# FFN gain applied behind the gather, and layer 1's embedding rows transposed earlier as filling

## The chip, the cores and the metric

The kernel runs on one core of one Trainium2 chip. The metric is the device time of one execution in microseconds. A core has TensorE (matrix products and transposes, PE in the profile, its weight loads PEld), VectorE (DVE), ScalarE (ACT), GpSimd (POOL), SyncE (SP, which issues most transfers) and 16 DMA engines. Each engine runs its own list of instructions in order; semaphores join the lists.

## The reference, cut to what matters

A trunk of two layers over 256 tokens of width 1024, all in f32. Each layer has a token mixer, a channel mixer (layer 0 dense, layer 1 experts), and an embedding that is gated and added:

```python
x = x + merged @ w_o[i]
h2 = rms_norm(x, g_ffn[i])           # x * rstd * g_ffn, per token
x = x + moe_swiglu(h2, w_router, wg, wu, wd)   # layer 1: top 2 of 8 experts
gate_p = sigmoid(rms_norm(x, g_ple[i]) @ w_ple_gate[i])
x = x + gate_p * (p[i] @ w_ple_up[i])
```

## The kernel before, in words

Products are made to about f32 precision from two parts of each operand: a high part that ScalarE rounds (`w_hi`, `hT_hi`, `inner_hi`) and the remainder that VectorE subtracts (`w_lo`, `hT_lo`, `inner_lo`). For each tile TensorE does three products: high by high, high by low, low by high (L1440 to L1442; in another order of pieces L1447 to L1449). Weights stream in units of 128x2048 through six raw slots (SyncE, `load_unit`) and three slots of parts. `keep_up(used)` lets ScalarE (L564) or VectorE (L860) prepare units up to three beyond the unit `used`; a weight unit that is due is thus always a copy of 1.9 us on ScalarE and a subtraction of 2.3 us on VectorE ahead of TensorE's twelve products. The order on each engine is written out by hand; nothing is scheduled at run time.

The activations are the transposed side: x or h is transposed by TensorE into PSUM, ScalarE makes the high part with the norm's gain as its scale per partition (L577), VectorE the remainder with the same gain (L934).

The stretch around the change is layer 1's output projection and routing:

- `mixer(1)` on TensorE ends with four weight units of the output projection. The last is done in four pieces (token tile, half of the columns), and VectorE adds each piece to x (`add_to_x`, L1182). Ahead of the fourth piece TensorE transposes the first half of x (`flip_x(4, 0)`, L1455).
- `route()` on TensorE multiplies x by the router's weights (L1452), transposing the second half of x and layer 1's p rows (`flip_p(1)`, L1488) in the middle. The logits go to VectorE, back through TensorE, and VectorE chooses two experts a token (`chosen`, L1227). TensorE counts places; VectorE makes the slot picks (`make_picks`, L1297), reads the number of items into a register (L1245) and makes the gates (L1248 to L1253).
- Products of p with `w_ple_up` (`ple_up_tile`, unit UP1) are placed between these steps as filling: eight tiles of three products.
- `gather_first` picks the rows of the first item: products of `normed` with `pick`, 32 of them, which come out transposed. `normed` is x times the FFN gain (`gain_x`, L1188, on VectorE, from a broadcast copy `gain_rows` that GpSimd loads, L544), times `rstd` (ScalarE, L748). ScalarE copies each half of the result (L757), VectorE subtracts (`gathered_low`, L866).
- The expert loop runs once per item (eight here), 42 weight units each. Near its end TensorE transposes the next item's rows (`x_slots`, loaded from `x_rows`, which holds `normed`), ScalarE copies them in two halves (L786) and VectorE subtracts (L866); the next item's first products wait for them.
- Behind the loop TensorE spreads the last item's rows, VectorE adds them to x (L1374), and the gated embedding of layer 1 follows.

Of the kernel before, what the change touches and what calls it, by code (L numbers as in the profile page):

```python
# [33 lines left out]
ALU = mybir.AluOpType  # L34
# [7 lines left out]
P = 128  # L42
# [15 lines left out]
def build_trunk(nc, x_in, p_in, lb_logits, g_mix, w_in, q_norm, k_norm, sinks, hgrn_norm, w_pa, w_pb, w_o,  # L58
# [89 lines left out]
    P_BANK = [4, 7]  # L148
# [12 lines left out]
    with ExitStack() as ctx:  # L161
# [23 lines left out]
        gain_rows = wide[:, 2048:3072]  # L185
# [8 lines left out]
        x_gained = deep[:, 3072:5120].rearrange("p (t n) -> p t n", t=TILES)  # L194
# [115 lines left out]
        gains_loaded = sem("gains_loaded")  # L310
        x_gained_ready = sem("x_gained_ready")
# [164 lines left out]
        def _(pool):  # L476
# [59 lines left out]
            for layer in range(DEPTH):  # L536
# [5 lines left out]
                if layer:  # L542
                    pool.wait_ge(merged_transposed, 4 * DEPTH)
                    pool.dma_start(gain_rows, g_ffn[layer:layer + 1, :].to_broadcast([P, D])).then_inc(gains_loaded, 16)  # L544
                    nc.gpsimd.memset(y_rows, 0.0).then_inc(item_y_ready, 2)
# [7 lines left out]
        def _(act_e):  # L553
# [17 lines left out]
            def norm(n, gain, used, items=0):  # L571
# [27 lines left out]
                elif n == 4:  # L599
# [4 lines left out]
                    take_p(1)  # L604
# [138 lines left out]

            def experts():
                act_e.wait_ge(rstd_ready, 5)
                for t in range(TILES):
                    act_e.wait_ge(x_gained_ready, t + 1)
                    nc.scalar.activation(normed[:, t, :], x_gained[:, t, :], ACT.Copy,  # L748
# [6 lines left out]
                for half in range(2):  # L755
                    act_e.wait_ge(gathered, half + 1)
                    nc.scalar.activation(hT[0][:, 4 * half:4 * half + 4, 0:P],  # L757
                                         banks(GATE + half).rearrange("p (k s) -> p k s", k=4),
                                         ACT.Copy).then_inc(gatheredT_high, 4)
# [4 lines left out]
                with act_e.Fori(0, count) as t:  # L764
# [19 lines left out]
                    for half in range(2):  # L784
                        act_e.wait_ge(gathered, t * 2 + 3 + half)
                        nc.scalar.activation(hT[0][:, 4 * half:4 * half + 4, 0:P],  # L786
                                             banks(GATE + half).rearrange("p (k s) -> p k s", k=4),
                                             ACT.Copy).then_inc(gatheredT_high, 4)
# [49 lines left out]
            mixer(1)  # L838
            norm(4, FFN_GAIN + KD, UP1)
# [4 lines left out]
        def _(dve):  # L844
# [205 lines left out]
            def mixer(layer):  # L1050
# [119 lines left out]
                keep_up(base + WO_AT + GATE_UNITS - 2)  # L1170
                add_to_x(WO1_OUT if layer else WO0_OUT, 4, base + WO_AT + GATE_UNITS, 3 * layer + 1, FFN_GAIN + layer * KD)
# [11 lines left out]

            def gain_x(t):

                dve.wait_ge(gains_loaded, 16)
                dve.wait_ge(x_updated, 4 * WO1_OUT + 3 + t)
                nc.vector.tensor_tensor(x_gained[:, t, :], x[:, t, :], gain_rows, ALU.mult).then_inc(x_gained_ready, 1)  # L1188
# [24 lines left out]
            def route():  # L1213
# [14 lines left out]
                gain_x(1)  # L1228
# [17 lines left out]

# [719 lines left out]
```

## Time and profile before

| what | value |
|---|---|
| median of 3 runs | 1655.76 us (1655.68 to 1656.78) |
| the profiled execution's own time | 1657.48 us |
| its span in the trace | 1655.5 us |
| TensorE matmul rows busy | 1632.7 us |
| VectorE busy | 1301.6 us |
| ScalarE busy | 1095.5 us |
| GpSimd busy | 80.2 us |

The span is what the trace covers; the execution's own time has 2.0 us around it. A matmul row is longer than its slot in the stream, since matmuls overlap. The idle time ahead of an instruction stands in brackets with what released it. The views below are of this one execution, and all starts are microseconds from its start.

### The profile page before, as it was taken

The page shows a single profiled execution, that of the slowest core. Times are in us where ns is not written, and L with a number is a line of the kernel's source. Part 1 is how long each engine was busy: PE and PEld are TensorE (multiplying, and loading weights), DVE is VectorE, ACT ScalarE, POOL GpSimd, SP SyncE. Part 2 cuts the span into 40 slices and gives each one's busy share as a digit, 9 for nine tenths or more (in the row PEclk, how much of TensorE's full clock was granted, in tenths as well). Part 3 has the DMA queues.
Part 4 walks back from the last instruction along what each step waited for, and adds up shares of the span by engine and source line. Part 5 has one row for each costly group of instructions (what it writes and reads, how often), then busy time and mean ns, then how long its engine had stood idle before and what let it go on. Part 6 is the DMA issues. An engine that isn't in the chain of part 4 may idle for free.

```text
span 1655.5 us, 21529 instructions
## 1 busy us (share of the span) xinstructions
PE 1632.7 (99%) x8189; PEld 1341.7 (81%) x8189; DVE 1301.6 (79%) x1091; ACT 1095.5 (66%) x901; POOL 80.2 (5%) x69
## 2 busy tenths in 40 slices
PE   7999999999999999999999999999999999999998
PEld 6878888888888887788888888888888888888886
DVE  6786754545578776898898988998988988888886
ACT  5556544343555655777777778778778778778774
POOL 0100000000001001100000000000000000000100
PEclk9999999999999999999999999999999999999999
DMA  8534456555364444999999999999999999999991
GB/s 313 174 132 153 154 203 196 184 179 202 144 205 140 153 153 155 373 396 367 376 395 356 381 394 343 395 393 345 393 394 345 394 393 343 396 392 349 394 400 51
DMA packets 201824, 479.98 MB, mean 290 GB/s; under 512 B 8816, under 2 KB 11440, under 8 KB 201776
## 3 DMA queue, kind: packets, MB, share of 16 engines
q1 hardware_dynamic: 198224, 466.20, 77.2%
q0 software_dynamic: 3552, 13.11, 2.9%
q8 instruction: 34, 0.56, 0.1%
q14 instruction: 14, 0.11, 0.0%
HBM read 470.89 MB, written 8.39 MB: 290 GB/s over the span
## 4 chain that ended last, share of the span: by engine, by line
PE 92%; DVE 5%; issue 1%; ACT 1%; DMA 0%; SPq 0%; DVEq 0%; ACTq 0%
PE ps L1440 28%; PE ps L1442 28%; PE ps L1441 28%; PE ps L1452 2%; DVE w_lo L860 2%; PE ps L1856 2%; PE ps L1449 1%; PE ps L1448 1%; PE ps L1447 1%; PE ps L1455 1%; DVE arena L952 0%; PE ps L1888 0%; PE ps L1738 0%; ACT normed L643 0%; PE ps L1599 0%
## 5 line engine op out<-in xcount | busy, mean ns | idle before, releaser
L860 DVE TENSOR_TENSOR w_lo<-raw,w_hi 128x2048 fp32r<-128x2048 f32 x442 | 1007.1, 2290 | 221.2 <-ACT w_hi L564 219.5
L564 ACT ACTIVATE w_hi<-raw 128x2048 fp32r<-128x2048 f32 x442 | 846.6, 1918 | 339.2 <-PE ps L1442 326.8
L1440 PE MATMUL ps<-w_hi,hT_hi 128*128 128x512 f32 (+1 forms) x1544 | 609.1, 394 | 3.6 <-DVE w_lo L860 1.8
L1442 PE MATMUL ps<-w_hi,hT_lo 128*128 128x512 f32 (+1 forms) x1544 | 599.5, 388 | 0.0
L1441 PE MATMUL ps<-w_lo,hT_hi 128*128 128x512 f32 (+1 forms) x1544 | 598.8, 388 | 0.0
L1440 PEld LDWEIGHTS ps<-w_hi,hT_hi 128*128 128x128 f32 x1544 | 290.5, 188 | 69.5 <-DVE w_lo L860 7.1
L1442 PEld LDWEIGHTS ps<-w_hi,hT_lo 128*128 128x128 f32 x1544 | 290.3, 188 | 61.0
L1441 PEld LDWEIGHTS ps<-w_lo,hT_hi 128*128 128x128 f32 x1544 | 290.8, 188 | 56.0
L1440 PE MATMUL ps<-w_hi,inner_hi 128*128 128x512 f32 x592 | 233.9, 395 | 0.0
L1442 PE MATMUL ps<-w_hi,inner_lo 128*128 128x512 f32 x592 | 230.8, 390 | 0.0
L1441 PE MATMUL ps<-w_lo,inner_hi 128*128 128x512 f32 x592 | 230.5, 389 | 0.0
L1440 PEld LDWEIGHTS ps<-w_hi,inner_hi 128*128 128x128 f32 x592 | 111.1, 188 | 24.4 <-DVE w_lo L860 1.8
L1442 PEld LDWEIGHTS ps<-w_hi,inner_lo 128*128 128x128 f32 x592 | 111.1, 188 | 23.6
L1441 PEld LDWEIGHTS ps<-w_lo,inner_hi 128*128 128x128 f32 x592 | 111.2, 188 | 22.1
L866 DVE TENSOR_TENSOR inner_lo<-ps,inner_hi 128x512 fp32r<-128x512 f32 x70 | 47.4, 685 | 26.1 <-ACT inner_hi L726 13.3
L628 ACT ACTIVATE arena<-ps,rstd 128x512 f32<-128x512 f32 (+1 forms) x40 | 24.5, 662 | 38.2 <-PE ps L1442 38.1
L1336 DVE SCALAR_TENSOR_TENSOR arena<-arena,slot_now,ps 128x512 f32<-128x512 f32 x56 | 41.5, 742 | 0.0
L767 ACT ACTIVATE inner_hi<-ps 128x512 fp32r<-128x512 f32 x56 | 33.1, 592 | 9.9 <-PE ps L1856 9.9
L1452 PE MATMUL ps<-arena 128*64 128x64 f32 (+4 forms) x616 | 36.8, 248 | 0.1
L521 POOL TENSOR_TENSOR pool_spare<-minus_half 128x1 f32<-128x1 f32 x8 | 10.4, 1304 | 524.3 <-ACT arena L796 523.1
L1452 PEld LDWEIGHTS ps<-arena 128*64 128x64 f32 (+2 forms) x616 | 29.9, 149 | 7.3 <-issue 5.7
L1856 PE MATMUL ps<-ident,arena 128*128 128x128 f32 x224 | 33.9, 273 | 0.0
(251 smaller groups left out, 821.7 us busy)
## 6 DMA issues: line engine op xcount, KB each, us to landing
raw<-in_w_moe_gate SPq DMA_DIRECT2D x112, 1024.0 KB, 8.2
raw<-in_w_moe_up SPq DMA_DIRECT2D x112, 1024.0 KB, 8.6
raw<-in_w_moe_down SPq DMA_DIRECT2D x112, 1024.0 KB, 8.3
raw<-in_w_in SPq DMA_DIRECT2D x38, 1024.0 KB, 6.0
raw<-in_w_dense_gate SPq DMA_DIRECT2D x14, 1024.0 KB, 5.1
raw<-in_w_dense_up SPq DMA_DIRECT2D x14, 1024.0 KB, 5.2
raw<-in_w_dense_down SPq DMA_DIRECT2D x14, 1024.0 KB, 4.9
raw<-in_w_o SPq DMA_DIRECT2D x8, 1024.0 KB, 4.8
```

What stands on the lines that cost most here:

```text
L564: nc.scalar.activation(w_hi[:, n % SLOTS, :], raw[:, n % RAW_SLOTS, :], ACT.Copy).then_inc(high_ready, 1)
L628: nc.scalar.activation(dst(t), src, func, scale=rstd[:, t:t + 1]).then_inc(proj_taken, 1)
L767: nc.scalar.activation(innerT[0][:, :, s % 2 * P:(s % 2 + 1) * P], banks(TRA).rearrange("p (k t) -> p k t", k=4), ACT.Copy).then_inc(item_ ...
L860: nc.vector.tensor_tensor(w_lo[:, n % SLOTS, :], raw[:, n % RAW_SLOTS, :], w_hi[:, n % SLOTS, :].bitcast(F32), ALU.subtract).then_inc(low_ ...
L866: return nc.vector.tensor_tensor(part[1][cols], full, part[0][cols].bitcast(F32), ALU.subtract)
L1336: nc.vector.scalar_tensor_tensor(act[s % 2], act[s % 2], slot_now[:, 0:1], banks(UP), ALU.mult, ALU.mult).then_inc(item_act, 1)
L1440: nc.tensor.matmul(o, x_parts[0][x_cols], parts[0], start=first, stop=False)
L1441: nc.tensor.matmul(o, x_parts[0][x_cols], parts[1], start=False, stop=False)
L1442: return nc.tensor.matmul(o, x_parts[1][x_cols], parts[0], start=False, stop=last)
L1447: nc.tensor.matmul(o, x_parts[0][x_cols], parts[0], start=first, stop=False)
L1452: return nc.tensor.matmul(o, lhsT, rhs, start=start, stop=stop)
L1856: last = nc.tensor.transpose(banks(TRA)[:, k * P:(k + 1) * P], act[s % 2][:, k * P:(k + 1) * P], ident[:, :])
```

## The change

The FFN gain of layer 1 is no longer multiplied into x's rows ahead of the gather. `normed` becomes x times `rstd`, and the gain is applied where the gathered rows stand transposed: the gain is then one value a partition, but another one for each of the eight column tiles, so the copy of a half (128x512) becomes four of 128x128 on ScalarE, and the subtraction of a half four on VectorE, in `experts()` ahead of the loop and in the loop. GpSimd's load of `gain_rows` and VectorE's two `gain_x` go.

Layer 1's p rows are transposed ahead of the last unit of the output projection, into bank 3 in place of bank 7. ScalarE copies them after `mixer(1)`, VectorE subtracts them ahead of `add_to_x`. The filling products are dealt out anew: three ahead of `flip_x(4, 1)`, six behind it, three ahead of the turn of the logits, nine ahead of the places, three ahead of the gather, none behind it. VectorE prepares weight unit MOE + 0 ahead of the gates (`keep_up(UP1 - 1)`).

```diff
-    P_BANK = [4, 7]
+    P_BANK = [4, 3]
...
-                    pool.dma_start(gain_rows, g_ffn[layer:layer + 1, :].to_broadcast([P, D])).then_inc(gains_loaded, 16)
...
                     high(range(4, KD))
-                    take_p(1)
                     squares(1)
...
+            def gathered_high(half):
+
+                for k in range(4 * half, 4 * half + 4):
+                    nc.scalar.activation(hT[0][:, k, 0:P], banks(GATE, 2)[:, k * P:(k + 1) * P], ACT.Copy,
+                                         scale=params[:, FFN_GAIN + KD + k:FFN_GAIN + KD + k + 1]).then_inc(gatheredT_high, 1)
...
-                    act_e.wait_ge(x_gained_ready, t + 1)
-                    nc.scalar.activation(normed[:, t, :], x_gained[:, t, :], ACT.Copy,
+                    nc.scalar.activation(normed[:, t, :], x[:, t, :], ACT.Copy,
...
-                    nc.scalar.activation(hT[0][:, 4 * half:4 * half + 4, 0:P],
-                                         banks(GATE + half).rearrange("p (k s) -> p k s", k=4),
-                                         ACT.Copy).then_inc(gatheredT_high, 4)
+                    gathered_high(half)
...
             mixer(1)
+            take_p(1)
             norm(4, FFN_GAIN + KD, UP1)
...
                 keep_up(base + WO_AT + GATE_UNITS - 2)
+                if layer:
+                    split_p(1)
                 add_to_x(WO1_OUT if layer else WO0_OUT, 4, base + WO_AT + GATE_UNITS, 3 * layer + 1, FFN_GAIN + layer * KD)
...
-                gain_x(1)
...
+                keep_up(UP1 - 1)
                 dve.wait_ge(route_exps, TILES)
...
-            def gathered_low(half):
-                dve.wait_ge(gatheredT_high, 4 * half + 4)
-                low(hT, banks(GATE + half).rearrange("p (k s) -> p k s", k=4),
-                    (slice(None), slice(4 * half, 4 * half + 4), slice(0, P))).then_inc(gatheredT_ready, 1)
+            def gathered_low(half, earlier=0):
+                dve.wait_ge(gatheredT_high, earlier + 4 * half + 4)
+                for k in range(4 * half, 4 * half + 4):
+                    last = nc.vector.scalar_tensor_tensor(hT[1][:, k, 0:P], banks(GATE, 2)[:, k * P:(k + 1) * P],
+                                                          params[:, FFN_GAIN + KD + k:FFN_GAIN + KD + k + 1],
+                                                          hT[0][:, k, 0:P].bitcast(F32), ALU.mult, ALU.subtract)
+                last.then_inc(gatheredT_ready, 1)
...
-            gain_x(0)
             norm_low(4, FFN_GAIN + KD, range(4, KD))
-            split_p(1)
             embedding(1, experts())
...
                 n = 3 * layer + 1
+                if layer:
+                    flip_p(1)
                 last_unit(base + WO_AT, GATE_UNITS - 1, GATE_UNITS, hT, 4, ready=mergedT_ready, ready_at=4 * layer,
...
                     if k == 4:
+                        pe.wait_ge(pT_ready, 2)
+                        ple_up_tile(0, [(0, 0)])
                         flip_x(4, 1)
-                        flip_p(1)
+                        ple_up_tile(0, [(1, 0), (0, 1)])
...
-                pe.wait_ge(pT_ready, 2)
-                ple_up_tile(0, [(0, 0)])
+                ple_up_tile(0, [(1, 1)])
...
-                ple_up_tile(0, [(0, 1), (1, 0), (1, 1)])
+                ple_up_tile(1, [(0, 0), (1, 0), (0, 1)])
...
                 route()
-                ple_up_tile(1, [(0, 0), (0, 1)])
+                ple_up_tile(1, [(1, 1)])
                 pe.wait_ge(normed_ready, TILES)
                 gather_first()
-                ple_up_tile(1, [(1, 0), (1, 1)])
```

## Rows read from the trace of the kernel before

**Rows 1.** The page: busy us, share of the span, instructions by engine.

```profile
PE 1632.7 (99%) x8189; PEld 1341.7 (81%) x8189; DVE 1301.6 (79%) x1091; ACT 1095.5 (66%) x901; POOL 80.2 (5%) x69
```

**Rows 2.** TensorE's waits, whole span: us in total, times, longest.

```profile
PE ps L1440 <- DVE w_lo L860: 1.8, 2, 1.1
...
PE ps L1455 <- DVE x L1374: 0.8, 1, 0.8
```

**Rows 3.** TensorE's timeline, output projection and routing: start us, us, what [idle before].

```profile
642.75 1.04 PE L1455 MATMUL ps<-ident,x 128*128 128x128 f32 x8
643.54 0.47 PE L1447 MATMUL ps<-w_hi,hT_hi 128*128 128x512 f32 x1
...
646.57 1.09 PE L1455 MATMUL ps<-ident,x 128*128 128x128 f32 x8
647.50 0.60 PE L1488 MATMUL ps<-ident,p_tok 128*128 128x128 f32 x4
649.06 0.29 PE L1452 MATMUL ps<-hT_hi,router_parts 128*16 128x256 f32 x1 [0.97 <-DVE hT_lo L934]
...
662.51 0.50 PE L1440 MATMUL ps<-w_hi,hT_hi 128*128 128x512 f32 x1 [0.71 <-DVE w_lo L860]
...
669.51 0.50 PE L1440 MATMUL ps<-w_hi,hT_hi 128*128 128x512 f32 x1 [1.10 <-DVE w_lo L860]
```

**Rows 4.** ScalarE's timeline, the same stretch.

```profile
638.92 1.92 ACT L564 ACTIVATE w_hi<-raw 128x2048 fp32r<-128x2048 f32 x1 [3.52 <-PE ps L1442]
...
648.70 0.62 ACT L569 ACTIVATE inner_hi<-ps 128x512 fp32r<-128x512 f32 x1
```

**Rows 5.** VectorE's timeline, the same stretch.

```profile
641.58 0.69 DVE L1182 TENSOR_TENSOR x<-x,ps 128x512 f32<-128x512 f32 x1 [0.67 <-PE ps L1449]
...
645.83 0.68 DVE L1182 TENSOR_TENSOR x<-x,ps 128x512 f32<-128x512 f32 x1
...
649.71 0.68 DVE L866 TENSOR_TENSOR inner_lo<-ps,inner_hi 128x512 fp32r<-128x512 f32 x1
...
653.78 1.22 DVE L1188 TENSOR_TENSOR arena<-x,arena 128x1024 f32<-128x1024 f32 x1
654.93 0.17 DVE L1233 SCALAR_TENSOR_TENSOR place<-ps,chosen 128x16 f32<-128x16 f32 x1
...
658.43 0.17 DVE L1248 TENSOR_TENSOR gate_w<-gate_w,chosen 128x16 f32<-128x16 f32 x1 [0.86 <-ACT gate_w L752]
...
667.16 6.70 DVE L860 TENSOR_TENSOR w_lo<-raw,w_hi 128x2048 fp32r<-128x2048 f32 x3 [0.23 <-DVE slot_now L1305]
```

**Rows 6.** The chain that ended last, routing: start us, us, what.

```profile
657.57 0.47 DVEq L1245
```

**Rows 7.** VectorE's timeline, layer 0's mixer.

```profile
131.35 2.16 DVE L1120 SCALAR_TENSOR_TENSOR arena<-ps,head_rstd,arena 128x128 f32<-128x128 f32 x8 [1.75 <-POOL head_rstd L501]
```

**Rows 8.** ScalarE's timeline, boundary of items 0 and 1.

```profile
781.10 1.92 ACT L564 ACTIVATE w_hi<-raw 128x2048 fp32r<-128x2048 f32 x1 [0.99 <-PE ps L1442]
```

**Rows 9.** VectorE's timeline, boundaries 0 to 1 and 1 to 2, and behind the loop.

```profile
782.38 1.28 DVE L866 TENSOR_TENSOR hT_lo<-ps,hT_hi 128x512 fp32r<-128x512 f32 x2
783.57 2.29 DVE L860 TENSOR_TENSOR w_lo<-raw,w_hi 128x2048 fp32r<-128x2048 f32 x1
...
902.11 1.28 DVE L866 TENSOR_TENSOR hT_lo<-ps,hT_hi 128x512 fp32r<-128x512 f32 x2
...
1623.83 1.88 DVE L1374 TENSOR_TENSOR x<-x,ps 128x512 f32<-128x512 f32 x3
```

**Rows 10.** TensorE's timeline, boundary of items 0 and 1, and behind the loop.

```profile
783.62 0.39 PE L1440 MATMUL ps<-w_hi,hT_hi 128*128 128x512 f32 x1
...
786.34 0.39 PE L1440 MATMUL ps<-w_hi,hT_hi 128*128 128x512 f32 x1
...
791.83 0.50 PE L1440 MATMUL ps<-w_hi,hT_hi 128*128 128x512 f32 x1
...
1625.26 1.06 PE L1455 MATMUL ps<-ident,x 128*128 128x128 f32 x8 [0.81 <-DVE x L1374]
```

More of the change, by code:

```diff
@@ L184, in build_trunk @@
         x_slots = wide[:, 1024:2048]
-        gain_rows = wide[:, 2048:3072]
         y_rows = wide[:, 3072:4096]
@@ L193, in build_trunk @@
         deep = arena[:, 7680:12800]
-        x_gained = deep[:, 3072:5120].rearrange("p (t n) -> p t n", t=TILES)
         ple_up = deep[:, 1024:3072].rearrange("p (t n) -> p t n", t=TILES)
@@ L309, in build_trunk @@
         out_pieces = sem("out_pieces")
-        gains_loaded = sem("gains_loaded")
-        x_gained_ready = sem("x_gained_ready")
         counted = sem("counted")
@@ L785, in experts @@
                         act_e.wait_ge(gathered, t * 2 + 3 + half)
-                        nc.scalar.activation(hT[0][:, 4 * half:4 * half + 4, 0:P],
-                                             banks(GATE + half).rearrange("p (k s) -> p k s", k=4),
-                                             ACT.Copy).then_inc(gatheredT_high, 4)
+                        gathered_high(half)
                     keep_up(MOE + PER_ITEM - 1, t)
@@ L1182, in add_to_x @@
                     nc.vector.tensor_tensor(xv, xv, banks(bank + 2 * t + half), ALU.add).then_inc(x_updated, 1)
[L1184 to L1188, printed above, removed]
             def dense():
@@ L1362, in experts @@
                     for half in range(2):
-                        dve.wait_ge(gatheredT_high, KD * (t + 1) + 4 * half + 4)
-                        low(hT, banks(GATE + half).rearrange("p (k s) -> p k s", k=4),
-                            (slice(None), slice(4 * half, 4 * half + 4), slice(0, P))).then_inc(gatheredT_ready, 1)
+                        gathered_low(half, KD * (t + 1))
                     keep_up(MOE + PER_ITEM - 1, t)
```

## The prediction

> **What bounds the kernel now.** I read the page first: TensorE's matmul rows fill 99% of the span [rows 1], so a microsecond in which TensorE stands still is a microsecond of the kernel, and little can be won. The view of waits says how little: behind the start, TensorE waits for VectorE's weight remainders (`w_lo`) twice, 1.8 us together, and for the summed rows at the end for 0.8 us [rows 2]; 0.97 us more stands in the routing stretch [rows 3]. All the standing time that this change could take away lies there, between 638 and 670 us. Then I read the timelines of TensorE, ScalarE and VectorE through that stretch [rows 3 to 5], the chain that ended last through its VectorE part [rows 6], and one item boundary of the expert loop [rows 8 to 10], because the changed scaling runs there too, eight times.
>
> Of the routing stretch the reader should see three things. The p transposes (L1488, four of them at 647.50) stand ahead of a wait of 0.97 us for `hT_lo` [rows 3]: they cost nothing there. From L1233 at 654.93 on, VectorE works almost without a pause to the third `w_lo`, whose wait ends TensorE's idleness at 669.51 [rows 3, 5]. And VectorE's one pause, 0.86 us ahead of L1248, is labelled ScalarE's exponentials, but the chain puts the time to L1245, VectorE's own register load of the item count [rows 5, 6]. So here VectorE's work sets the end, not TensorE's and not the missing filling.
>
> **The change, part by part.** Times are of the profiled execution.
>
> *Transposes of p into the output projection.* TensorE gives a product a slot of 2.72 / 12 = 0.227 us (783.62 to 786.34 for twelve [rows 10]). Eight transposes take 642.75 to 643.54, and the product behind them shows 0.47 us where one in the stream shows 0.39, a restart of 0.08: 0.87 us for eight, 0.43 for four [rows 3]. They leave idle time, where they cost nothing, and go ahead of the last unit, where TensorE has no pause: +0.43. Behind them ScalarE copies p (0.62 us, the row of L569) when its weight copy at 638.92 is done, 638.92 + 1.92 = 640.84, so to about 641.4 [rows 4]. VectorE's `split_p(1)` waits for that, 0.68 us to 642.1 (the row of L866 at 649.71), and now stands ahead of the additions to x, whose second began at 641.58 [rows 5]. Two additions follow at 0.6 us apart, to 643.27. The x transposes need them and would come at 642.75 + 0.43 = 643.18. TensorE takes some 0.15 us to act on a VectorE result (second addition's end 1623.83 + 0.60 + 0.68 = 1625.11, transposes at 1625.26 [rows 9, 10]), so they start at 643.42: +0.67.
>
> *One filling product group ahead of `flip_x(4, 1)`.* The last addition to x ends at 645.83 + 0.68 + 0.67 = 647.18 [rows 5], and the router products end in step with it, at 646.57 + 0.67 = 647.24 [rows 3]. So x is ready just as TensorE comes, and the three products put in between take 3 × 0.227 + 0.11 = 0.80 us of the path (0.11 is the restart behind other work, 0.50 for 0.39 at 791.83 [rows 10]): transposes at 648.04, +1.47. The six products behind the transposes, 1.5 us, go into the pause that ended at 649.06, now at 650.5; they hide. Everything that follows by dependency comes 1.47 later: the logits, the choice, L1233 at 656.40. The filling between logits and choice has the same count as before (3, then 9 products), so nothing is won back.
>
> *The gain multiplies go.* `gain_x(0)` lies in VectorE's wait for ScalarE: nothing. `gain_x(1)`, 1.22 us at 653.78, ends as TensorE's place counts arrive: it covers their way, and L1233 could hardly start before 654.93 without it [rows 5]. Nothing, at best 0.1. The gather could start earlier by its rows, but it waits for `picks_ready`, which is VectorE's. Its gain rows, one POOL DMA and its broadcast, were not waited for by anybody: nothing.
>
> *The gain on transposed slots.* Each half was one 128x512 subtraction on VectorE, two of them 1.28 us [rows 9]; now it is four scalar-tensor-tensors of 128x128 from PSUM. Eight of those take 2.16 us, 0.26 apart [rows 7]: +0.88 us on VectorE for each set of eight slots' tiles. On ScalarE eight small copies with a scale take, if spaced like VectorE's (my estimate), about 2.2 us for some 1.2; ScalarE pauses 0.99 us behind them, ahead of its copy at 781.10 [rows 8], so this hides. The Trainium skill, page "Perfetto Trace Analysis", section "Optimizing Scalar/DVE Operations", gives about 125 ns as VectorE's extra for each instruction on PSUM; by that the six more would cost 0.75, an estimate, and each 0.88 below would be 0.75. The trace has the form itself, so 0.88 stands.
>
> *Routing, the sum.* VectorE's path from L1233 to the end of the third `w_lo` keeps its parts in another order: `keep_up(UP1 - 1)` only moves one `w_lo` (2.29 us [rows 9]) ahead of the gates, and since the pause there is the register load ahead of it, it fills nothing. So +1.47 for the later start and +0.88 for the two halves: the third `w_lo` ends 2.35 later, and TensorE, idle for it before, starts at 671.86 for 669.51. **Routing: +2.35.** Bounds: if the pause can be filled (0.4) and the additions don't wait (0.24), and the filling hides by half (0.4), 1.3; if the gates, now behind a weight remainder, hold TensorE as well, 3.2.
>
> *Each boundary between items, seven.* Before: `hT_lo` runs 782.38 to 783.66, the next unit's `w_lo` 783.57 to 785.86; TensorE takes the slots at 783.62 and that unit at 786.34 [rows 9, 10]. So there is 0.5 us of room at either place, less than 0.88. After: the first half is ready at 782.38 + 3 × 0.26 + 0.34 = 783.50, just in time, a lost 0.1 at most; the `w_lo` ends at 786.74, TensorE starts the unit at 786.80 for 786.34 and loses 0.11 more in the restart: +0.58. The restart at 791.83 [rows 10], 0.11 and a little waiting, falls away, but ScalarE's next copy waits for the later unit and hands 0.1 on. **+0.5 each, seven times: +3.5.** Bounds: 0.2 (half of the room turns out larger) and 0.88 (all of it comes through), so 1.4 to 6.2.
>
> *Behind the last item.* `w_lo` and the additions to x run back to back on VectorE, additions at 1623.83 [rows 9], and TensorE waits 0.8 us for them [rows 2]. **+0.88**, bounds 0.4 and 0.9.
>
> Sum: 2.35 + 3.5 + 0.88 = +6.7 us. On the profiled execution's 1657.48 (span 1655.5 and 2.0 around it) that is 1664.2; that execution is 1.7 above the median of the runs, 1655.76, so for a median **1662.5**. The bounds add to 3.1 and 10.3.
>
> **The rivals.**
> - *Hidden at the boundary.* If VectorE's 0.88 fits the boundary (smaller spacing, or later pauses absorb it), 2.35 less what fills, say 1.6, + 0.35 + 0.6 = +2.6: 1658.3. For it: VectorE is busy for 79% of the span only [rows 1]. Against: both rooms are 0.5 us. Chance 0.15.
> - *Everything passes.* 2.35 + 8 × 0.88 = +9.4: 1665.2, or more if the stalls also delay ScalarE's copies a second time. Chance 0.15.
> - *Faster.* The mechanism is the removed multiply: if the places arrive well ahead of 654.93, VectorE's path loses 1.15, and with the filling in place the three waits of this stretch (0.97, 0.71, 1.10 [rows 3]) all go, and 0.7 us of restarts: at best −3.5 and 1652.3, with nothing lost at the boundaries. It decides only if the path gives more than the 1.47 + 0.88 put on it. Chance 0.03.
> - *Smaller pieces end sooner.* For each boundary, shorter instructions could let the first slots be used earlier; here TensorE is signalled only by the last of four, and is not waiting, so it gives nothing to win: at the very best the boundary is free and routing 1.3, +1.9: 1657.7. Chance 0.02. The same section of "Perfetto Trace Analysis" in the Trainium skill says that breaking instructions up may finish work sooner where the engine is not saturated but leaves others bubbles.
>
> **The numbers.** The forecast itself, slower with stalls at each boundary, has 0.65 and its own range 1659.5 to 1665. The range takes in most of the hidden and of the everything case: 1657.9 to 1666. Of no change means within 0.2%, 3.3 us, about what a measurement of this kernel can tell: the hidden case, the pieces case and a little of the forecast's low tail: 0.2. Faster by more: 0.03. Slower by more: 0.77.
>
> **What would show it.** In the changed profile: the x transposes near 643.4 and 648.0; L1233's counterpart near 656.4; the wait for the third `w_lo` ending near 671.9; eight small scalar-tensor-tensors of about 2.16 us at each boundary, and behind four of TensorE's products a new wait of about 0.4 us for `w_lo`, with item periods of 120.2 for 119.7 us (782.38 to 902.11 [rows 9]); TensorE's wait for x at the end still near 0.8. I am wrong if the spacing of the small instructions is below 0.2 us, if item periods stay at 119.7, or if the place counts turn out to have waited for the multiply.

## The result and the profile after

The changed kernel takes 1665.65 us (median of 6 runs, 1662.11 to 1665.9) where the kernel before, run beside it, takes 1656.27 (6 runs, 1655.04 to 1659.11): ratio 1.005, 95% interval 1.004 to 1.006. The change makes the kernel slower by about 9 us on these medians. The profiled execution took 1665.9 us, with a span of 1664.0, so 8.5 of span over before. Compared once more with other runs beside it (below, `after_again`) the ratio was 1.0040 [1.0026, 1.0054], 6 us on the medians. Executions of this one kernel differ by 4 us, for two reasons that the sections below separate; 6 to 9 us is what the runs support.

The page of the changed kernel, the row that answers to [rows 1]: TensorE 5.4 us more for the same 8189 products, VectorE 5.6 us more in 52 more instructions, ScalarE 54 more.

```profile
PE 1638.1 (98%) x8189; PEld 1343.4 (81%) x8189; DVE 1307.2 (79%) x1143; ACT 1104.4 (66%) x955; POOL 99.3 (6%) x68
```

TensorE's waits, which answer to [rows 2]. The two waits for `w_lo` have shrunk to 0.5 us in all. In their place stand 2.4 us for the gates and 1.5 us behind the slot table, and the wait for x at the end has doubled from 0.8 to 1.7.

```profile
PE ps L1443 <- DVE slot_columns L1245: 2.4, 1, 2.4
...
PE ps L1446 <- DVE x L1367: 1.7, 1, 1.7
...
PE ps L1431 <- DVE hT_lo L1302: 1.5, 1, 1.5
PE ps L1431 <- DVE w_lo L856: 0.5, 3, 0.2
```

TensorE's timeline through the stretch of [rows 3]. The p transposes (L1479) open it; x follows at 643.13 and 647.61; then the gather, the slot table, and expert products.

```profile
638.50 0.60 PE L1479 MATMUL ps<-ident,p_tok 128*128 128x128 f32 x4
...
643.13 1.09 PE L1446 MATMUL ps<-ident,x 128*128 128x128 f32 x8
...
647.61 1.04 PE L1446 MATMUL ps<-ident,x 128*128 128x128 f32 x8
...
656.79 3.81 PE L1443 MATMUL ps<-arena,normed 128*128 128x128 f32 x32 [0.20 <-DVE arena L1289]
663.03 0.40 PE L1443 MATMUL ps<-slot_columns,arena 128*64 128x2 f32 x8 [2.43 <-DVE slot_columns L1245]
664.90 0.79 PE L1431 MATMUL ps<-w_hi,hT_hi 128*128 128x512 f32 x1 [1.47 <-DVE hT_lo L1302]
665.49 0.63 PE L1432 MATMUL ps<-w_lo,hT_hi 128*128 128x512 f32 x1
665.91 0.63 PE L1433 MATMUL ps<-w_hi,hT_lo 128*128 128x512 f32 x1
...
671.26 0.40 PE L1431 MATMUL ps<-w_hi,hT_hi 128*128 128x512 f32 x1
```

The last lines hold what I had not foreseen: from 664.90 products start 0.43 us apart, fourteen of them, where they stood 0.23 apart before. The windows of the same kernel say why. The columns are start:end, length, busy us (instructions) of PE, PEld, DVE, ACT, POOL, then the granted clock, DMA share and GB/s.

```profile
660.60:664.90 4.30, 0.40 (x8) 0.32 (x9) 4.13 (x12) 4.25 (x7) 0.00 (x0) 0.91 1.03 368
664.90:671.10 6.20, 6.20 (x15) 4.92 (x16) 5.43 (x21) 1.57 (x2) 1.35 (x2) 0.51 0.97 340
...
786.25:906.51 120.26, 120.11 (x550) 98.05 (x549) 107.37 (x77) 92.82 (x69) 8.95 (x4) 1.00 1.02 375
```

TensorE was busy for 0.40 of the 4.30 us ahead, and then worked 6.2 us at a granted clock of 0.51, the 1.2 GHz level instead of 2.4. The third window is one item: 120.26 us where [rows 9] gave 119.73.

VectorE's timeline, for [rows 5 and 7]: the choice of rows at L1224 (L1233 before), the pause ahead of the moved `w_lo` at 659.77, eight small instructions in two groups, and the third `w_lo` at 669.74, ending at 672.03.

```profile
655.74 0.17 DVE L1224 SCALAR_TENSOR_TENSOR place<-ps,chosen 128x16 f32<-128x16 f32 x1 [1.10 <-PE ps L1443]
...
659.77 2.29 DVE L856 TENSOR_TENSOR w_lo<-raw,w_hi 128x2048 fp32r<-128x2048 f32 x1 [1.40 <-issue]
...
663.12 1.13 DVE L1302 SCALAR_TENSOR_TENSOR hT_lo<-ps,params,hT_hi 128x128 fp32r<-128x128 f32 x4
...
669.74 2.29 DVE L856 TENSOR_TENSOR w_lo<-raw,w_hi 128x2048 fp32r<-128x2048 f32 x1 [0.59 <-DVE slot_now L1297]
...
786.25 2.16 DVE L1302 SCALAR_TENSOR_TENSOR hT_lo<-ps,params,hT_hi 128x128 fp32r<-128x128 f32 x8
788.32 4.49 DVE L856 TENSOR_TENSOR w_lo<-raw,w_hi 128x2048 fp32r<-128x2048 f32 x2
```

The chain that ended last, where [rows 6] had 0.47 us for the register load of the item count: the load's part in the chain is now 1.01 us.

```profile
658.37 1.01 DVEq L1236
```

TensorE at the boundary of items 0 and 1, and behind the loop, for [rows 10]: the slots are taken at 787.50, 1.25 behind the first small instruction (1.24 before), and the next unit at 790.66, 3.16 later instead of 2.72. The row shows only 0.15 of that 0.44 as idle time, since a row is longer than its slot.

```profile
787.50 0.49 PE L1431 MATMUL ps<-w_hi,hT_hi 128*128 128x512 f32 x1
...
790.66 0.50 PE L1431 MATMUL ps<-w_hi,hT_hi 128*128 128x512 f32 x1 [0.15 <-DVE w_lo L856]
...
1633.71 1.06 PE L1446 MATMUL ps<-ident,x 128*128 128x128 f32 x8 [1.68 <-DVE x L1367]
```

**Where the time went.** The executions differ ahead of the change by up to 2.6 us. In eight of the fourteen profiled ones (all kernels together) eight to eleven products at the kernel's start run at the low clock, and the anchor named next lies at 637.58 to 638.66; in the other six none does, and it lies at 636.05 to 636.93. So I count from an anchor that both kernels have, the start of the output projection's last unit (with the p transposes where they are ahead of it): 638.66 before, 638.50 after. "First boundary" is the start of item 1's `hT_lo`; the loop is the seven periods from there to the last `hT_lo`; the rest is the tail.

| us from the anchor | before | after | difference |
|---|---|---|---|
| x transposes, first / second | 4.09 / 7.91 | 4.63 / 9.11 | +0.54 / +1.20 |
| choice of rows on VectorE | 16.27 | 17.24 | +0.97 |
| first expert product | 23.85 | 26.40 | +2.55 |
| third `w_lo` ready | 30.79 | 33.53 | +2.74 |
| third unit on TensorE | 30.85 | 34.81 | +3.96 |
| first boundary | 143.72 | 147.75 | +4.03 |
| seven periods | 838.06 | 841.76 | +3.70 |
| tail | 35.06 | 35.99 | +0.93 |

4.03 + 3.70 + 0.93 = 8.66, less 0.16 for the earlier anchor: the 8.5 of span.

### The profile page after: what moved, and what is told of

Read it like the earlier page. It is cut to its first block, busy times and chain, and to the rows that moved or that the text cites. A ratio compares the mean times of both kernels' runs of the same rounds, so it can differ in the third digit from the quotient of the medians.

```text
span 1664.0 us, 21614 instructions
## 1 busy us (share of the span) xinstructions
PE 1638.1 (98%) x8189; PEld 1343.4 (81%) x8189; DVE 1307.2 (79%) x1143; ACT 1104.4 (66%) x955; POOL 99.3 (6%) x68
## 4 chain that ended last, share of the span: by engine, by line
PE 87%; DVE 8%; issue 3%; ACT 1%; DMA 0%; DVEq 0%; SPq 0%; ACTq 0%
PE ps L1431 27%; PE ps L1433 26%; PE ps L1432 26%; DVE w_lo L856 3%; PE ps L1443 2%; PE ps L1849 1%; DVE hT_lo L1302 1%; PE ps L1440 1%; PE ps L1439 1%; PE ps L1438 1%; PE ps L1446 1%; DMA raw<-in_w_in 0%; DVE arena L948 0%; PE ps L1731 0%; ACT normed L637 0%
## 5 line engine op out<-in xcount | busy, mean ns | idle before, releaser
L517 POOL TENSOR_TENSOR pool_spare<-minus_half 128x1 f32<-128x1 f32 x8 | 32.0, 3996 | 526.6 <-ACT arena L791 523.1
```

Source lines behind the costliest of these rows:

```text
L517: nc.gpsimd.tensor_tensor(pool_spare[:, :], minus_half[:, 0:1], minus_half[:, 0:1], ALU.add).then_inc(spare_written, 1)
```

## The experiments

Two questions: which of the change's two halves carries which loss, and why the first stretch lost 4.0 us where I had put 2.35. All times below are from the anchor unless a row says otherwise, and from one profiled execution each. The runs came in three groups, each with its own runs of the kernel before: the first four kernels against a median of 1656.91, the next four against 1655.42, the last four against 1656.59.

### The two halves: gain_only and order_only

`gain_only` is the kernel before with the gain moved to the transposed slots, all else in the old order (the edit is shown in part). `order_only` is its complement: the p transposes, the filling and the early `w_lo` moved, the gain still multiplied on the rows.

```diff
# gain_only
-            gain_x(0)
...
-                gain_x(1)
...
-                            low(hT, banks(GATE + half)...).then_inc(gatheredT_ready, 1)
+                    gathered_low(half, KD * (t + 1))
# order_only
+                if layer:
+                    flip_p(1)
...
+                        ple_up_tile(0, [(0, 0)])
                         flip_x(4, 1)
+                        ple_up_tile(0, [(1, 0), (0, 1)])
...
+                keep_up(UP1 - 1)
                 dve.wait_ge(route_exps, TILES)
```

> The kernel before with the first half of the change alone: gain behind the transposes, filling and p transposes as before. My theory (eight small VectorE instructions cost 0.88 us a set): item periods 120.26 us as in the changed kernel, for 119.73 before, so 7 x 0.53 = 3.7; 0.88 behind the last item; 0.88 in the routing, where six filling products still stand behind the gather and the granted clock stays at 1.00. Sum +5.5 us. Rival (the boundaries' loss comes from the later start or the other order, not from the small instructions): periods 119.7, sum 0 to +1.

> The second half alone: p transposed in the output projection, filling dealt out anew, one weight remainder ahead of the gates; the gain multiplied ahead of the gather as before. My theory: item periods 119.73 and nothing lost behind the last item; the head 1.0 later, VectorE's third w_lo 1.5 to 2 later, and, as TensorE has no filling behind the gather and waits for the gates, a stretch at the lower clock as in the changed kernel: +3.1 us in all, 1.9 if the clock stays up. With gain_only this adds to the change's 8.5. Rival (the halves work on each other): the two sums miss 8.5 by more than 1.

Measured: `gain_only` 1661.87, ratio 1.0036 [1.0022, 1.0050]; first boundary 145.64 (+1.92), periods 841.66 (+3.60), tail 35.91 (+0.85). `order_only` 1659.21, ratio 1.0015 [1.0005, 1.0025]; first boundary 145.63 (+1.91), periods 838.14 and tail 34.98, as before. So the boundaries and the tail belong to the gain half alone, and the sum over both, 1.92 + 3.60 + 0.85 + 1.91 + 0.08 − 0.08 = 8.3, is near the change's 8.66. The third `w_lo` adds up too: 1.90 later by the one, 0.92 by the other, 2.74 by both in one kernel.

Two things missed. In `gain_only` VectorE's pauses grew, 0.86 to 1.36 and 0.23 to 0.59, so the first stretch cost a microsecond more than its 0.88. And the clock fell in both, for seven and six products; in `gain_only`, where I had expected it to stay up, one wait of 1.83 us for the first unit's `w_lo` went ahead of that. There TensorE still waits 0.47 us for the third `w_lo`, so the clock cost nothing there; in `order_only` it has no wait left, its third unit begins at 32.65 with the `w_lo` ready at 31.71, so 0.9 of its 1.9 us are the clock's.

```profile
669.33 0.50 PE L1429 MATMUL ps<-w_hi,hT_hi 128*128 128x512 f32 x1 [0.47 <-DVE w_lo L856]
```

(TensorE's timeline of `gain_only`, the third unit.)

### The clock: kept_warm, kept_warm_half and both again

The changed kernel with identity products into parts of two banks that hold nothing at that time, in TensorE's two waits, so that it does not stand idle; `kept_warm_half` has ten and five for the twenty and twelve. They are added work whose results nobody reads.

```diff
                 gather_first()
+                for _ in range(20):
+                    mm(banks(TRB)[:, 3 * P:4 * P], ident[:, :], ident[:, :], True, True)
                 pe.wait_ge(gates_ready, 1)
...
                 pe.wait_ge(counted, 1)
+                for _ in range(12):
+                    mm(banks(TRA)[:, 3 * P:4 * P], ident[:, :], ident[:, :], True, True)
                 count = pe.value_load(...)
```

> The changed kernel, and TensorE fills its two waits behind the gather with 20 and 12 products of the identity with itself, whose results nobody reads. My theory (the idle wait lowered the clock, and the fourteen products at 0.43 us kept TensorE behind the third w_lo): granted clock 1.00 all through the first unit, first expert product still near 664.9, third unit near 672.1 for 673.3, so -1.2 us against the changed kernel. Rival 1 (the third w_lo sets the time anyway): 0. Rival 2 (the clock falls for another reason, in spite of the products): the slots stay at 0.43, 0 or slower.

Measured: 1665.83, ratio 1.0053 [1.0036, 1.0070]; no slow product, but first boundary 148.03. The size was wrong. TensorE's timeline of `kept_warm`: a 128x128 product of `f32` is two rows of some 0.115 us, so twenty were forty, and the filling ended at 667.60, later than the wait it was to fill.

```profile
660.00 4.63 PE L1443 MATMUL ps<-ident 128*128 128x128 f32 x40
664.57 0.40 PE L1443 MATMUL ps<-slot_columns,arena 128*64 128x2 f32 x8
664.89 2.94 PE L1443 MATMUL ps<-ident 128*128 128x128 f32 x24
667.60 0.48 PE L1431 MATMUL ps<-w_hi,hT_hi 128*128 128x512 f32 x1
```

It shows that the clock stays up when TensorE is kept from idling, and nothing of the cost. Hence half as many:

> The changed kernel with 10 and 5 unread identity products in TensorE's two waits behind the gather (the 20 and 12 of the last try were two matmul rows each and ran 2.7 us past the wait they were to fill). Measured from the p transposes, so that the earlier part of the run does not count. My theory (idle time lowered the clock): slots of 0.23 us from the first expert product, the third unit 33.6 behind the p transposes for 34.8, first item boundary 1.2 us sooner than in the changed kernel. Rival (VectorE's third w_lo sets the time anyway): 34.8 and no gain.

Measured: 1662.13, ratio 1.0036 [1.0023, 1.0050]. No slow product; the first expert product still at 26.40, the third `w_lo` still at 33.45, but the first boundary at 146.39 against 147.75. TensorE's timeline of `kept_warm_half`: full slots from the start, and a wait for the third `w_lo` again.

```profile
663.33 0.49 PE L1431 MATMUL ps<-w_hi,hT_hi 128*128 128x512 f32 x1 [0.24 <-issue]
663.66 0.39 PE L1432 MATMUL ps<-w_lo,hT_hi 128*128 128x512 f32 x1
...
670.44 0.50 PE L1431 MATMUL ps<-w_hi,hT_hi 128*128 128x512 f32 x1 [1.36 <-DVE w_lo L856]
```

So in the profiled execution of the changed kernel the low clock cost 1.36 us, and the filling has no other effect up to there. Does every execution pay it? I ran both side by side:

> The changed kernel itself, again, beside the others of this call. In the first profile fourteen products of the first two expert units ran at 0.43 us; in profiles of three kernels with nearly the same routing it was seven or eight, and there the time was 1.2 to 1.3 us less up to the first boundary. My theory: the length of the stretch at the lower clock differs between executions of one kernel; measured from the p transposes the first boundary is at 146.4 with some eight slow products, or at 147.7 with fourteen, and the items' periods (120.25) and the end (36.0) don't move. Rival: the changed kernel always has fourteen, and the other kernels' differences shortened it.

> The kernel of kept_warm_half again, timed beside the changed kernel on one chip. If the lower clock costs the changed kernel 1.3 us in most executions, this is 1.3 us faster in the median; if only in few, 0 to 0.5. In the profile no slow product behind the gather, first boundary at 146.4 either way.

Measured: `after_again` 1662.69, ratio 1.0040 [1.0026, 1.0054], first boundary 147.87 with fourteen slow products; `kept_warm_again` 1663.91, ratio 1.0046 [1.0033, 1.0060], first boundary 146.41 with none. The profiles repeat to 0.1 us, but the medians do not show the 1.4 us.

In the profiled executions without filling the count was 6 to 8 in five variants, 9 in one, 12 in one, and 14 twice in the changed kernel itself. `vector_small` (below) has the changed kernel's order on TensorE and VectorE, the same first expert product within 0.1 us, and eight slow products: its first boundary stands at 146.42. So seven or eight hide behind the third `w_lo`, and the 1.36 us are the price of fourteen.

How often does the changed kernel meet the fourteen? Of the executions without a profile only the span and the mean granted clock are on record, but the parts are known: the anchor (636.05 to 636.93 with no slow product at the kernel's start, 637.58 to 638.66 with eight or more), 146.4 or 147.8 to the first boundary, 841.8 and 36.0. As an estimate, a span is thus 1660.2 to 1661.1 with neither stretch, 1663.1 to 1664.2 with slow products at the start and fourteen behind the gather, and 1661.6 to 1662.8 with one of the two. Of the changed kernel's eleven executions five have spans of 1663.5 to 1664.0 and a granted clock of 0.998, four have 1660.0 to 1660.6 and 0.999, and two lie between (1662.1 and 1661.7). So at least four did not pay the 1.36 us, and five most likely did: without it, 1663.5 would need an anchor of 639.3 or later, and of the 46 executions of the kernel before that ran beside these variants only one had a span that asks for that. This also says why the medians of the pair above are no test of it: four spans of `kept_warm_again` are 1661.8 to 1662.7, which without fourteen slow products means a slow start, while three of `after_again` (1660.0 to 1660.6) had neither.

### VectorE's order and its pauses: gates_first and stores_later

`gates_first` takes back the early weight remainder; `stores_later` makes POOL wait for the gates before it stores x and the normed rows.

```diff
# gates_first
-                keep_up(UP1 - 1)
                 dve.wait_ge(route_exps, TILES)
# stores_later
                 pool.wait_ge(normed_ready, TILES)
+                pool.wait_ge(gates_ready, 1)
                 pool.dma_start(x_sum[0:SEQ, ...
```

> The changed kernel without keep_up(UP1 - 1) ahead of the gates, which puts that weight remainder back behind the gates. My theory: the gates come 2.2 us earlier (near 660.8), the slot table with them, so TensorE's idle stretch is cut in two; the first expert product then waits for its w_lo, near 664.3 for 664.9. VectorE's third w_lo ends where it did. If the clock then stays up, -1.2; if it falls all the same, -0.6 to 0. Rival (the early w_lo was a help): +1 or more.

> The changed kernel, and GpSimd waits for the gates before it issues its four stores of x and normed, so that no transfer runs while VectorE loads the item count. My theory (the stores, started 1.5 us earlier by the change, slow VectorE's register loads): the pause behind L1258 falls from 1.40 to 0.86 us and the one ahead of the third w_lo from 0.59 to 0.23; routing 0.5 to 0.9 us shorter. Rival 1 (the pauses come from VectorE's changed instructions): 1.40 and 0.59 stay. Rival 2: the later stores reach the raw loads or the item's scatter and the run is slower.

Measured, `gates_first`: 1662.81, ratio 1.0039 [1.0025, 1.0054]; first expert product 25.76, third `w_lo` 33.50 as after, seven slow products, all hidden, first boundary 146.41. The early `w_lo` gains nothing on VectorE. On TensorE it delays the gates by 2.2 us, so that the slot table stands in the middle of the idle stretch and the first expert product comes 0.64 later (26.40 for 25.76). That is lost only if the low clock lasts: `vector_small`, with the early `w_lo` and eight slow products, has its first boundary at 146.42 as well. So the 1.34 us that this run's first boundary gains over the changed kernel are the shorter slow stretch, and not shown to be the order's doing.

The delayed gates bear on the 1.47 in after's row at 664.90. The row names `hT_lo`, but in `scalar_small` (below), where `hT_lo` comes sooner, the first product stands at the same 26.43 and the row says `[1.54 <-issue]`. So it is not `hT_lo`. What lies there is TensorE's own load of the item count into a register, which stands behind the slot table in its list and so behind the gates (ready at 662.98). The view of its source line has it. These are TensorE's loads of the kernel before, of after and of `stores_later` (ns, start us):

```profile
L1842 PEldq TENSOR_LOAD <-n_items_i x1: 1118/1118/1118, 659.5 to 659.5; - x1
...
L1835 PEldq TENSOR_LOAD <-n_items_i x1: 1177/1177/1177, 663.0 to 663.0; - x1
...
L1836 PEldq TENSOR_LOAD <-n_items_i x1: 504/504/504, 660.0 to 660.0; - x1
```

In after it runs from 663.0 to 664.2, two register instructions behind it end at 664.5, and the product follows at 664.90. Before, the load was as long, 1.12 us, but ran from 659.5 on while TensorE worked through six filling products, and nothing waited for it. Taking these six away from behind the gather laid it bare; I had overlooked that.

Measured, `stores_later`: 1663.52, ratio 1.0045 [1.0029, 1.0060]. VectorE's timeline: the first pause shrinks from 1.40 to 0.74, the second stays 0.59; the chain has 0.35 for the load where after has 1.01.

```profile
656.74 2.29 DVE L857 TENSOR_TENSOR w_lo<-raw,w_hi 128x2048 fp32r<-128x2048 f32 x1 [0.74 <-issue]
...
666.71 6.70 DVE L857 TENSOR_TENSOR w_lo<-raw,w_hi 128x2048 fp32r<-128x2048 f32 x3 [0.59 <-DVE slot_now L1298]
```

VectorE's own load of the count, before, after and in `stores_later`:

```profile
L1245 DVEq TENSOR_LOAD <-n_items_i x1: 662/662/662, 657.4 to 657.4; - x1
...
L1236 DVEq TENSOR_LOAD <-n_items_i x1: 1208/1208/1208, 658.2 to 658.2; - x1
...
L1237 DVEq TENSOR_LOAD <-n_items_i x1: 547/547/547, 655.8 to 655.8; - x1
```

The third `w_lo` comes 0.70 sooner (32.83) and the first boundary at 145.80. The first pause is thus shown: the register load takes longer while POOL's stores are under way. The change issues them from 655.05 to 657.9, all four ahead of VectorE's load; before, they were issued from 656.50 on, and only the first was out. The DMA engines were busy for 0.34 of the load's time before, for 0.99 of it in after, and not at all in `stores_later`. `order_only`, where the stores come later again, has 0.68 us for the load, and `gain_only`, where they come early, 1.17. It is the stores and not the traffic as such: in `kept_warm` TensorE's load, at 665.7 just after the stores had landed, took 0.49 us with the DMA engines busy all the time with weights. TensorE's load is short in `stores_later` too (0.50), and the first expert product comes at 25.18 for 26.40. For the second pause my theory fell. The run's median does not follow the profile (1663.52 is within the changed kernel's 1662.69 to 1665.65): the profiled span is 1659.7, below all of the changed kernel's, and the other three are 1661.4 to 1661.7, as slow products at the start would make them. So this stays a result on the stretch, not on the kernel's time.

### The small instructions: vector_small and scalar_small

Each keeps the eight small instructions with the gain on one engine and goes back to two large ones without it on the other: in `vector_small` ScalarE's high parts lack the gain, in `scalar_small` VectorE subtracts without it.

```diff
# vector_small, ScalarE
-                for k in range(4 * half, 4 * half + 4):
-                    nc.scalar.activation(hT[0][:, k, 0:P], ..., scale=params[...]).then_inc(gatheredT_high, 1)
+                nc.scalar.activation(hT[0][:, 4 * half:4 * half + 4, 0:P],
+                                     banks(GATE + half)..., ACT.Copy).then_inc(gatheredT_high, 4)
# scalar_small, VectorE
-                for k in range(4 * half, 4 * half + 4):
-                    last = nc.vector.scalar_tensor_tensor(...)
+                last = low(hT, banks(GATE + half)..., (slice(None), slice(4 * half, 4 * half + 4), slice(0, P)))
```

> The changed kernel with ScalarE's copies in halves again (without the gain, which only the remainders then have) and VectorE's remainders in eight pieces. My theory (the boundary's loss is VectorE's): item periods 120.25 as in the changed kernel, 0.9 lost behind the last item, the same time within 0.5 us. Rival (ScalarE's eight copies cost it too): periods between 119.73 and 120.25.

> The changed kernel with ScalarE's copies in eight pieces with the gain, and VectorE's remainders in two halves again (subtracting without the gain, so the low parts are not the remainders). My theory: item periods 119.73 as before the change, 35.1 behind the last boundary for 36.0, so 4.6 us less than the changed kernel with routing another 0.9 less. For the second pause of VectorE, ahead of its third w_lo (0.59 for 0.23 in every kernel with the gain moved): if it is VectorE's own eight instructions that lengthen it, 0.23; if not, 0.59. Rival (ScalarE's small copies cost part of the boundary): periods above 119.8.

Measured: `vector_small` 1662.28, ratio 1.0041 [1.0026, 1.0056]: periods 841.77, tail 35.97, both as after. `scalar_small` 1660.45, ratio 1.0020 [1.0011, 1.0029]: periods 838.07, tail 35.08, both as before. The loss of 3.70 + 0.93 is VectorE's eight small instructions; ScalarE's cost nothing. VectorE's timeline of `scalar_small`:

```profile
658.81 2.29 DVE L856 TENSOR_TENSOR w_lo<-raw,w_hi 128x2048 fp32r<-128x2048 f32 x1 [1.41 <-issue]
...
667.54 2.29 DVE L856 TENSOR_TENSOR w_lo<-raw,w_hi 128x2048 fp32r<-128x2048 f32 x1 [0.23 <-DVE slot_now L1297]
...
785.15 1.27 DVE L862 TENSOR_TENSOR hT_lo<-ps,hT_hi 128x512 fp32r<-128x512 f32 x2
```

The second pause is back at 0.23, so its 0.36 more goes with VectorE's small instructions too (how, no run tells); the first stays at 1.41, as the stores have it. The third `w_lo` is ready at 32.25, 1.3 sooner, yet the first boundary stands at 147.57: twelve slow products, the third unit at 34.58. Here the clock, not the `w_lo`, sets the end of the stretch.

### The filling: flip_first, and the version before with an early remainder: early_lo

`flip_first` puts the second x transposes ahead of all three filling groups (nine products) that stood around them. `early_lo` is the kernel before with one weight remainder in the place of `gain_x(0)`, which moves behind the copy of the logits.

```diff
# flip_first
-                        pe.wait_ge(pT_ready, 2)
-                        ple_up_tile(0, [(0, 0)])
                         flip_x(4, 1)
-                        ple_up_tile(0, [(1, 0), (0, 1)])
+                        pe.wait_ge(pT_ready, 2)
+                        ple_up_tile(0, [(0, 0), (1, 0), (0, 1)])
# early_lo
-            gain_x(0)
+            keep_up(UP1 - 1)
             norm_low(4, FFN_GAIN + KD, range(4, KD))
...
                 ....then_inc(logits_copied, 1)
+                gain_x(0)
                 dve.wait_ge(logits_turned, 1)
```

> The changed kernel with its first three filling products behind flip_x(4, 1) in place of ahead of it. My theory (x is ready when TensorE comes, so the filling is on the path): the second x transposes 8.4 behind the p transposes for 9.1, the places' read (L1224) near 16.5 for 17.2, and the third w_lo and the first boundary 0.5 to 0.7 sooner. Rival (x comes later than the router products end, so the filling was free): 9.1 and 17.2 stay, or the nine filling products behind the transposes now hold the router up by 0.7.

> The kernel before, with keep_up(UP1 - 1) in the place of gain_x(0), in VectorE's wait for ScalarE, and gain_x(0) moved behind the copy of the logits, in its wait for TensorE. My theory (VectorE's path from the choice to the third w_lo bounds the routing): the logits 0.5 later, the path 2.2 shorter, first expert product at about the old time, third unit 1.5 us sooner, nothing changed in the items: -1.5 us, 0.09%, too little for the timed ratio but plain in the profile. Rival (TensorE's own work or the clock bounds it): 0 or slower.

Measured, `flip_first`: 1663.34, ratio 1.0040 [1.0025, 1.0056]. The second transposes come at 8.50 for 9.11, the choice at 16.83 for 17.24, the third `w_lo` at 33.07 for 33.53. The product group ahead of the transposes was on the path, with 0.6 us at its place and 0.4 to 0.5 from the choice on.

Measured, `early_lo`: 1655.49, ratio 0.9997 [0.9988, 1.0006]. Its choice comes 0.5 later (16.77), but the third `w_lo` 1.65 sooner (29.14), no wait for it is left on TensorE, and the first boundary is at 142.12 for 143.72, with periods and tail unchanged. In the profile this version is 1.6 us ahead of the kernel before in that stretch; 0.1% is below what the timed runs can tell, so it is not shown to be faster.

## Why the prediction was right, and where its sum was short

The forecast, slower with a stall at each boundary, is what happened. In size it was short: 1665.65 for 1662.5, which is above the forecast's own range (1659.5 to 1665) and just inside the wide one (1657.9 to 1666). With `after_again`'s median, 1662.69, it would look exact, but that is luck, since the median depends on how many executions meet the slow stretches. In spans I had +6.7; the trace has +8.5, and some 7.3 where the slow products behind the gather hide. Step by step:

- **Transposes of p, late additions:** +0.67 predicted, +0.54 measured. Right.
- **The filling ahead of `flip_x(4, 1)`:** +0.80 predicted; the transposes went from 0.54 to 1.20 late, +0.66, and `flip_first` takes 0.61 away. Right in mechanism, a little high. Of the predicted 1.47 together, 0.27 were thus never lost, and 0.23 more were won back behind the transposes, since the choice of rows is 0.97 late. I had written that nothing is won back. The two timelines of TensorE show where it is: the turn of the logits starts 1.13 us behind the last router product before (650.21 to 651.34) and 0.91 after (651.20 to 652.11). Before, the filling product between them had to wait for the split of p, which VectorE ended at 650.39; after, it follows at once. That this wait is the cause is read from these rows; no run isolates it.
- **The gain multiplies:** nothing predicted. `gain_only` has the choice at 16.30 for 16.27 with `gain_x(1)` gone: it covered the way of the place counts, as argued.
- **The two halves in the routing stretch:** +0.88, and it is in the chain. But two pauses that I had carried over unchanged grew with it, 0.86 to 1.40 and 0.23 to 0.59. 0.97 + 0.88 + 0.54 + 0.36 = 2.75, the 2.74 of the third `w_lo`. So 2.35 was near by an error each way: 0.5 too much at its head, 0.9 too little in the pauses.
- **The early `w_lo`:** I wrote that it fills nothing; `gates_first` shows that (33.50 for 33.53). That it delays the gates I had only as a bound. The first product comes 0.64 us later (26.40 for 25.76), which costs time only where the slow stretch is long.
- **The routing term is the mis-sized one:** "TensorE, idle for it before, starts at 671.86 for 669.51", +2.35. It measured +3.96 at that unit in the profiled execution: 2.7 for the `w_lo` and 1.3 for the clock. The upper bound of 3.2 did not hold this either. What failed is that I priced TensorE's idle time as idle time alone; `kept_warm_half` shows that the products behind it paid as well, 1.36 us. With eight slow products the term is 2.70 (`vector_small`, first boundary 146.42 for 143.72) and inside the bounds. Nor did the sum have TensorE's register load, which the six filling products had hidden: it lengthens the idle stretch, while the end of the routing is still set by the third `w_lo` or the slow products.
- **Each boundary:** +0.5 each, 3.5 predicted; 0.53 each, 3.70 measured, the item period 120.26 for my 120.2. The first half was in time, as predicted, and the loss is ahead of the next unit, which comes 0.44 later behind it (the row at 790.66). `scalar_small` and `vector_small` show that it is VectorE's small instructions. The Trainium skill, page "Perfetto Trace Analysis", section "Optimizing Scalar/DVE Operations", would have put six more instructions at 0.75, an estimate from its 125 ns; the trace has 2.16 for 1.28, 0.88. Its other rule, that breaking instructions up may let work finish sooner, goes the other way here: VectorE signals only behind the last of four, and each item loses 0.53.
- **Behind the last item:** +0.88 predicted, +0.93 measured. But I also wrote that TensorE's wait for x would stay near 0.8, and it became 1.68. That contradicted my own sum: VectorE's 0.88 had to show up somewhere.
- **The rivals:** "hidden at the boundary" falls by the periods, "faster" by the choice of rows, "smaller pieces" by both. "Everything passes" was nearer in its total than the forecast, 9.4 against 8.5, but not in its mechanism: the boundaries gave 0.53 each, not 0.88. The rest of the way was the clock and the pauses.

## What to carry to other kernels

When a broadcast multiply is moved behind a transpose, where the gain lies along the partitions, one large instruction becomes one for each tile; read what the small form costs from a place where the kernel already has it, and ask at each repetition whether the next consumer has more room than that. Two 0.5 us rooms could not take 0.88 us, so the loss came once per item. Before work is taken out of a stretch in which the bottleneck engine waits, count that engine's idle microseconds as a risk for its clock too, and do not take a pause for a constant: it may be a register load, here twice as long while stores are under way. Filling products can also hide such a load on the bottleneck engine itself; look for one before they are moved.

## What the runs showed of the hardware

- **The clock after a short idle stretch.** TensorE busy for 0.40 of 4.30 us was followed by a granted clock of 0.51 over 6.20 us and 0.43 us slots for 0.23. In `gain_only` one wait of 1.83 us, with TensorE busy ahead of it, was followed by seven slow products (0.51 over 3.38 us); the wait of 0.71 us in the kernel before by none. With filling, no product was slow. Between executions the stretch varied: 6 to 14 products here, and none or 8 to 11 at the kernel's start. The Trainium skill, page "TensorE: Matmul & The Clock Gate", section "What's actually happening", says that the number of slow products at a kernel's start differs from run to run of the same kernel; the traces agree: one kernel, profiled as `kept_warm_half` and `kept_warm_again`, had none and eight there.
- **Register loads.** A load of the item count took 0.46 to 0.55 us with GpSimd's stores not yet begun or already landed, even with the DMA engines busy throughout with weights, and 1.05 to 1.25 us on VectorE, ScalarE and TensorE while the stores were under way; 0.66 to 0.72 on VectorE just after they began.
- **The name beside a wait.** After's 1.47 us ahead of the first expert product names `hT_lo`; the variant with an earlier `hT_lo` left the product where it was, and the view of the source line shows the engine's own load in that time.
- **Products of `f32`.** A 128x128 identity product is two rows of some 0.115 us.
